# One transformer kernel on Trainium2: inverse sums turned into rows on TensorE before their store, mem's reload behind a projection's slabs, first halves that end in the order of the second, one add on VectorE

## What is computed

```python
h_res = h_res + rms_norm(m @ w_o[i], post_norm_g[i])          # end of the first block
...
h = rmsnorm(x, ln1[l]);  z = h @ w_in[l]
s = einsum('bqhd,bkhd->bhqk', qi, k) * scale                  # forgetting attention, 8 heads of 64
s = s + (ci[..., :, None] - cT[..., None, :])                 # causal, c = cumsum(log_sigmoid(f))
p = softmax(s);  fx_out = einsum('bhqk,bkhd->bqhd', p, v)
x = x + concat([ml_out, fx_out], -1) @ w_out[l]
x = x + cross_attention(rmsnorm(x, ln_x[l]), rmsnorm(mem, ln_mem[l]), w_xq[l], w_xkv[l], w_xo[l])
u = relu(rmsnorm(x, ln2[l]) @ w_ff1[l]);  x = x + (u * u) @ w_ff2[l]
return rmsnorm(x, ln_f)
```

## Time and profile before

| | us |
|---|---|
| median of 3 runs | 2868.69 (2868.45 to 2870.37) |
| the profiled execution | 2866.0 |
| its span, first to last instruction | 2864.2 |
| PE busy, share of the span | 96% |
| PEld, DVE, ACT, POOL | 79%, 36%, 32%, 20% |
| TensorE's granted clock, mean | 0.989 |
| slab to w_hi on ACT (L1357), mean | 1.055 |
| slab to w_lo on POOL (L507), mean | 2.44 |

### The profile page before, as it was taken

How to read it: one execution, slowest core, us unless ns; L and a number is a source line. 1 busy time by engine, 2 the same in 40 slices (tenths; PEclk the granted TensorE clock), 3 DMA queues, 4 the chain that set the end, 5 groups by cost and what they waited for, 6 DMA issues and landing times.

```text
span 2864.2 us, 34206 instructions
## 1 busy us (share of the span) xinstructions
PE 2762.2 (96%) x13636; PEld 2269.4 (79%) x13636; DVE 1029.4 (36%) x1292; ACT 923.6 (32%) x1469; POOL 581.4 (20%) x246
## 2 busy tenths in 40 slices
PE   7999999999999999999999998899999999999999
PEld 6677788898888887777778887677688888888887
DVE  3544423553313222734534665221323212122223
ACT  4455531112222114433435554233423112021122
POOL 1000012221222223321011224231021222222221
PEclk9899999999999999999999999899999999999999
DMA  3000001111111114121113344320020111111112
GB/s 124 14 13 13 15 22 45 52 45 44 45 44 48 48 51 147 45 91 37 37 44 74 54 84 115 112 66 30 22 66 30 52 45 51 52 44 51 44 52 88
DMA packets 50966, 154.50 MB, mean 54 GB/s; under 512 B 13140, under 2 KB 13396, under 8 KB 50088
## 3 DMA queue, kind: packets, MB, share of 16 engines
q1 hardware_dynamic: 45904, 128.11, 15.2%
q10 hardware_dynamic: 4952, 24.82, 2.3%
HBM read 138.04 MB, written 10.67 MB: 52 GB/s over the span
## 4 chain that ended last, share of the span: by engine, by line
PE 48%; issue 38%; POOL 5%; DVE 3%; ACT 2%; DMA 2%; POOLq 0%; SPq 0%; DVEq 0%; ACTq 0%
PE ps L594 19%; PE ps L675 15%; PE ps L696 4%; POOL w_lo L507 4%; PE ps L1108 2%; DMA w_raw<-in_units 2%; PE ps L1066 1%; PE ps L1257 1%; PE ps L1060 1%; DVE fx_tl L2504 1%; PE ps L1145 1%; DVE stat L2495 1%; PE ps L1282 1%; PE ps L1166 1%; ACT fx_th L1866 1%
## 5 line engine op out<-in xcount | busy, mean ns | idle before, releaser
L507 POOL TENSOR_TENSOR w_lo<-w_raw,w_hi 128x1024 fp32r<-128x1024 f32 x205 | 500.1, 2440 | 2138.8 <-ACT w_hi L1357 2138.6
L594 PE MATMUL ps<-A_hi,w_hi 128*128 128x512 f32 (+1 forms) x1920 | 549.0, 372 | 7.5 <-POOL w_lo L507 1.5
L594 PE MATMUL ps<-A_lo,w_hi 128*128 128x512 f32 (+1 forms) x1920 | 545.3, 370 | 0.0
L594 PE MATMUL ps<-A_hi,w_lo 128*128 128x512 f32 (+1 forms) x1920 | 544.5, 370 | 0.0
L594 PEld LDWEIGHTS ps<-A_hi,w_hi 128*128 128x128 f32 x1920 | 341.8, 189 | 71.5 <-issue 6.2
L594 PEld LDWEIGHTS ps<-A_hi,w_lo 128*128 128x128 f32 x1920 | 343.4, 189 | 61.8
L594 PEld LDWEIGHTS ps<-A_lo,w_hi 128*128 128x128 f32 x1920 | 343.3, 188 | 61.5
L1357 ACT ACTIVATE w_hi<-w_raw 128x1024 fp32r<-128x1024 f32 x205 | 216.2, 1055 | 517.2 <-PE ps L675 331.2
L2572 DVE TENSOR_TENSOR X<-ps,X 128x512 f32<-128x512 f32 x96 | 66.4, 692 | 394.9 <-PE ps L675 317.1
L675 PE MATMUL ps<-w_hi,U_hi 128*128 128x512 f32 x448 | 174.3, 389 | 0.0
L675 PE MATMUL ps<-w_lo,U_hi 128*128 128x512 f32 x448 | 174.3, 389 | 0.0
(11 more groups left out here) (421 smaller groups left out, 4205.7 us busy)
## 6 DMA issues: line engine op xcount, KB each, us to landing
w_raw<-in_units SPq DMA_DIRECT2D x203, 512.0 KB, 3.5
X<-in_x ACTq DMA_DIRECT2D x4, 1024.0 KB, 11.6
X<-in_x ACTq DMA_DIRECT2D x1, 4096.0 KB, 14.9
x_spill<-X ACTq DMA_DIRECT2D x1, 4096.0 KB, 12.2
X<-x_spill ACTq DMA_DIRECT2D x1, 4096.0 KB, 15.9
out<-lnf_xn SPq DMA_DIRECT2D x8, 512.0 KB, 2.6
w_raw<-in_units SPq DMA_DIRECT2D x12, 256.0 KB, 2.5
negm_bc<-negm_rows ACTq DMA_DIRECT2D x4, 512.0 KB, 3.5
```

The source lines that it names most:

```text
L507: nc.gpsimd.tensor_tensor(w_lo[:, slot, :], w_raw[:, slot, :], w_hi[:, slot, :].bitcast(F32), ALU.subtract).then_inc(w_lo_ready, 1)
L594: last = nc.tensor.matmul(out, w[:, slot, o:o + m], v[:, k, cols] if k is not None else v[:, cols], start=(first and j == 0 and q == 0), s ...
```

## The change

Five edits, and the diff's core below.

1. **Inverse sums as rows.** After the last chunk of the first step of head h+1, PE transposes head h's 128 x 8 inverse sums into free columns of that chunk's bank (fx_row_turn; for head 7 after the last step's chunks). ACT copies the 8 x 128 result to fx_row (fx_row_copy). SP stores that: 8 rows of 128 floats (inverse_out waits for fx["row"]). DVE's inverse of head h waits for the transpose of head h-2, no longer for its store.
2. **SP's order.** inverse(h) is inverse_out(h) and inverse_in(h) together; inverse(h-1) stands in head h's turn, before copies(2h+3); inverse(5) before copies(15), inverse(6) after the load of n0+13, inverse(7) after the load of n0+17. The wait for fx["out"] and the two reloads of mem move behind the loads of w_out's eighth unit.
3. **POOL's order.** normalised(6) moves between the low parts of n0+14 and n0+15.
4. **Tiles of the first halves.** The last unit (kp 3) of w_o's, w_out's and w_xo's first half goes in the order TILES, ACT and DVE read the banks in that order, and the second half's tile o waits for o + 1 banks.
5. **Last add.** For the last tile DVE adds Y to X, before its ln1 scaling of the tile before; POOL's new_x(7) goes, and ACT's last stats waits for x_last.

```diff
@@ -294,6 +294,7 @@
 fx_inv = ar("fx_inv", 79872, [P, S])
+fx_row = ar("fx_row", 83968, [P, 2, P])
@@ -364,7 +365,7 @@
 fx = {k: sem(f"fx_{k}") for k in ("half", "q_hi", "q_lo", "dup0", "dup1", "sc", "nm", "p", "t", "ph", "pl", "vh", "vl", "pv",
-                                  "o", "inv", "inv_out", "inv_in", "out", "ones")}
+                                  "o", "inv", "row", "inv_out", "inv_in", "out", "ones")}
 mem_moved = sem("mem_moved")
@@ -376,6 +377,7 @@
 y_sq, y_cp, y_std, post_g_in, x_new = sem("y_sq"), sem("y_cp"), sem("y_std"), sem("post_g_in"), sem("x_new")
+x_last = sem("x_last")
 y_new = sem("y_new")
@@ -415,9 +417,8 @@
         def inverse_out(h):
-            sp.wait_ge(fx["inv"], h + 1)
-            sp.dma_start(inv_d[h % 2].rearrange("q p -> p q"), stat[:, 16 + 8 * (h % 2):24 + 8 * (h % 2)],
-                         allow_slow_non_contiguous=True).then_inc(fx["inv_out"], 16)
+            sp.wait_ge(fx["row"], h + 1)
+            sp.dma_start(inv_d[h % 2], fx_row[0:ST, h % 2, :]).then_inc(fx["inv_out"], 16)
@@ -441,35 +442,29 @@
         sp.wait_ge(mem_moved, 32)
+        def inverse(h):
+            inverse_out(h)
+            inverse_in(h)
...
             next_load(n0 + 4 + h)
+            if h:
+                inverse(h - 1)
             copies(2 * h + 3)
-            if h:
-                inverse_in(h - 1)
             copies(2 * h + 4)
...
                 sp.dma_start(mem_lo_a.bitcast(F32), meml_d.rearrange("p (a b) c -> p a (b c)", b=2)).then_inc(mem_moved, 16)
-            inverse_out(h)
         next_load(n0 + 10)
+        inverse(5)
         copies(15)
-        inverse_in(5)
-        next_load(n0 + 11)
-        next_load(n0 + 12)
-        inverse_out(6)
-        next_load(n0 + 13)
-        next_load(n0 + 14)
-        inverse_in(6)
-        next_load(n0 + 15)
-        next_load(n0 + 16)
-        inverse_out(7)
-        next_load(n0 + 17)
-        inverse_in(7)
-        sp.wait_ge(fx["out"], HEADS)
-        sp.wait_ge(mem_moved, 64)
-        sp.dma_start(mem_hi_x[:, :, :].bitcast(F32), memh_d).then_inc(mem_moved, 16)
-        sp.dma_start(mem_lo_x[:, :, :].bitcast(F32), meml_d).then_inc(mem_moved, 16)
+        for n in range(n0 + 11, n0 + 14):
+            next_load(n)
+        inverse(6)
+        for n in range(n0 + 14, n0 + 18):
+            next_load(n)
+        inverse(7)
@@ -481,6 +476,10 @@
                 load(n, n % 2, 1024)
+            sp.wait_ge(fx["out"], HEADS)
+            sp.wait_ge(mem_moved, 64)
+            sp.dma_start(mem_hi_x[:, :, :].bitcast(F32), memh_d).then_inc(mem_moved, 16)
+            sp.dma_start(mem_lo_x[:, :, :].bitcast(F32), meml_d).then_inc(mem_moved, 16)
         elif iterations == 1:
@@ -536,7 +535,6 @@
         new_x(o)
-    new_x(ST - 1)
     b = FIRST["w_xo"] + 4
@@ -565,9 +563,11 @@
             normalised(h - 1, n0 + h + 4)
-    for n in range(n0 + 10, n0 + 18):
+    for n in range(n0 + 10, n0 + 15):
         low(n, n % 2)
-    normalised(6, n0 + 18)
+    normalised(6, n0 + 15)
+    for n in range(n0 + 15, n0 + 18):
+        low(n, n % 2)
     normalised(7, n0 + 18)
@@ -983,7 +983,7 @@
             pe.wait_ge(sp_lo, SPLIT[split] + 2 * kp + 2)
-            sweep_unit(n0 + kp, (n0 + kp) % 2, kp, hi, lo, off, tiles=tiles, free=free)
+            sweep_unit(n0 + kp, (n0 + kp) % 2, kp, hi, lo, off, tiles=TILES if kp == 3 else tiles, free=free)
@@ -1006,7 +1006,7 @@
-    sweep_tiles(n0 - 4, wo_hi, wo_lo, A_hi, A_lo, META, lambda o: pe.wait_ge(y_cp, TILES[o] + 1),
+    sweep_tiles(n0 - 4, wo_hi, wo_lo, A_hi, A_lo, META, lambda o: pe.wait_ge(y_cp, o + 1),
                 lambda o: ln1_tile(o - 3) if o >= 3 else None)
@@ -1143,7 +1143,16 @@
                 last = nc.tensor.transpose(ps[:, 4 + g % 2, x * P:(x + 1) * P], fx_p[:, o:o + P], ident)
+            if s == 0 and c == 3 and h:
+                last = fx_row_turn(h - 1, g)
             last.then_inc(fx["t"], 1)
+    def fx_row_turn(h, g):
+        e = h % 2
+        pe.wait_ge(fx["inv"], h + 1)
+        return nc.tensor.transpose(ps[0:ST, 4 + g % 2, 384:512], stat[:, 16 + 8 * e:24 + 8 * e], ident)
@@ -1214,12 +1223,15 @@
             fx_fill(4 * h + s + 1)
+    pe.wait_ge(fx["pl"], FX_CHUNKS * HEADS - 1)
+    fx_row_turn(7, FX_CHUNKS * HEADS).then_inc(fx["t"], 1)
     fx_values(7, 3)
...
             pe.wait_ge(fx["pl"], FX_CHUNKS * HEADS)
+            pe.wait_ge(fx["row"], HEADS)
         if o == 6:
@@ -1231,7 +1243,7 @@
-    sweep_tiles(FIRST["w_out"] + 4, wout_hi, wout_lo, A_hi, A_lo, META, lambda o: pe.wait_ge(sw["w_out"], TILES[o] + 1),
+    sweep_tiles(FIRST["w_out"] + 4, wout_hi, wout_lo, A_hi, A_lo, META, lambda o: pe.wait_ge(sw["w_out"], o + 1),
                 lambda o: lnx_tile(o - 3) if o >= 3 else None)
@@ -1310,7 +1322,7 @@
-    sweep_tiles(n0 - 4, wxo_hi, wxo_lo, A_hi, A_lo, META, lambda o: pe.wait_ge(sw["w_xo"], TILES[o] + 1),
+    sweep_tiles(n0 - 4, wxo_hi, wxo_lo, A_hi, A_lo, META, lambda o: pe.wait_ge(sw["w_xo"], o + 1),
                 lambda o: ln2_tile(o - 3) if o >= 3 else None)
@@ -1680,12 +1692,12 @@
     feed(n0 + 8, n0 % 2, (n0 + 8) // 2)
-    for t in range(ST):
-        take_y(0, t, t)
+    for o, t in enumerate(TILES):
+        take_y(0, o, t)
     feed(n0 + 9, (n0 + 9) % 2, (n0 + 9) // 2)
...
     ln1 = Norm("ln1", lambda t: X[:, t, :], ln1_t, A_hi, TILES, 32, META, (2, 3),
-               ready=lambda o: act.wait_ge(x_new, o + 1))
+               ready=lambda o: act.wait_ge(x_new, o + 1) if o + 1 < ST else act.wait_ge(x_last, 1))
     for o, t in enumerate(TILES):
@@ -1852,6 +1864,14 @@
+    def fx_row_copy(h, g):
+        if h == 0:
+            act.wait_ge(mem_moved, 32)
+        if h >= 2:
+            act.wait_ge(fx["inv_out"], 16 * (h - 1))
+        fn(fx_row[0:ST, h % 2, :], ps[0:ST, 4 + g % 2, 384:512], ACT.Copy).then_inc(fx["row"], 1)
@@ -1863,6 +1883,8 @@
             w = HB if c < j else 384
+            if s == 0 and c == 3 and h:
+                fx_row_copy(h - 1, g)
             fn(fx_th[:, FX_T_AT[j] + c, 0:w], ps[:, 4 + g % 2, 0:w], ACT.Copy).then_inc(fx["ph"], 1)
@@ -1908,6 +1930,8 @@
     x_key(6)
+    act.wait_ge(fx["t"], FX_CHUNKS * HEADS + 1)
+    fx_row_copy(7, FX_CHUNKS * HEADS)
     split_hi(mix, lambda k: None, range(2, 4))
@@ -2350,8 +2374,11 @@
             v.tensor_tensor(X[:, TILES[0], :], X[:, TILES[0], :], Y[:, TILES[0], :], ALU.add).then_inc(x_new, 1)
-        else:
-            ln1.xn()
+            continue
+        if o + 1 == ST:
+            dve.wait_ge(y_new, ST)
+            v.tensor_tensor(X[:, TILES[o], :], X[:, TILES[o], :], Y[:, TILES[o], :], ALU.add).then_inc(x_last, 1)
+        ln1.xn()
     ln1.xn()
@@ -2521,7 +2548,7 @@
         if h >= 2:
-            dve.wait_ge(fx["inv_out"], 16 * (h - 1))
+            dve.wait_ge(fx["t"], FX_CHUNKS * (h - 1) + 4)
         v.reciprocal(stat[:, 16 + 8 * e:24 + 8 * e], stat[:, 80 + 8 * e:88 + 8 * e]).then_inc(fx["inv"], 1)
@@ -2575,7 +2602,7 @@
     lnx = Norm("lnx", lambda t: X[:, t, :], lnx_t, A_hi, A_lo, TILES, 32, META, LNX_PAIRS)
-    residual("w_out", 0, 0, FIRST["w_out"] + 3, tiles=range(ST))
+    residual("w_out", 0, 0, FIRST["w_out"] + 3)
@@ -2615,7 +2642,7 @@
     ln2 = Norm("ln2", lambda t: X[:, t, :], ln2_t, A_hi, A_lo, TILES, 0, META, LN2_PAIRS)
-    residual("w_xo", 0, 0, FIRST["w_xo"] + 3, tiles=range(ST))
+    residual("w_xo", 0, 0, FIRST["w_xo"] + 3)
```

## The result

The changed kernel takes 2843.52 us (median, 2843.15 to 2848.60), the kernel before, run beside it, 2869.53 (2868.45 to 2872.96): a ratio of 0.991, 95% interval 0.9895 to 0.992. Forecast were 2841.5 us. The profiled execution of after takes 2843.15 us, 22.85 less than that of before; forecast for that pair were 27.2. Most terms of the sum can be read off at their size, but 4.35 us of the gain are missing.

A forecast was written before the change was run, and what follows sets the result against it. PE's waits were taken as the bound. 2866.0 (profiled) - 21.5 + 1.0 - 5.5 - 1.2 = 2838.8, plus 2.7 for the median gives 2841.5 us; range 2836 to 2852 with (a) and (b).

The forecast's parts named there:

- Bound and cause: PE's waits bound the kernel; the longest, 17.4 us for a w_out slab's low part, comes from SP's queue.
- Part 1: Tail of SP's queue: w_out's third slab loads earlier, its first half runs without the wait; gain 21.5 us (19 to 22).
- Part 2: Heads: eight added inverse-row transposes on PE, with ACT copies; 1.0 us lost (0.3 to 3.2).
- Part 3: w_o: the first half's tile order lets the second half follow at once; gain 5.5 us (bound 3 to 5.5).
- Part 4: Last add on DVE: the low part PE awaits at L617 comes earlier; gain 1.2 us (0.8 to 2.6).
- POOL's move: normalised(6) ahead of three low parts, reading SBUF beside DVE's first split of mix; nothing counted, 2.4 us more at worst.
- later stages follow PE and shift whole: Stages after the edited ones were taken to start earlier by the full gain, with no term of their own.
- (a): Rows get in the heads' way: seven heads lose 0.8 us each, x_k's seventh slab 2 us late; 2849, chance 0.09.
- (b): w_o's wait stays in part as the feed before ACT's first copy slips; 5.5 us come back, 2847, chance 0.04.
- (c): Bandwidth, not SP's order, held w_out's slab, so nothing gained there: 2863; listed as 2866 for a median, chance 0.03.
- (d): Inverse-sums store stays slow and SP holds the heads: loss begins at 8.1 to 9.4 us of store; chance 0.02.
- The signs of being wrong: A new wait over 3 us in the heads, or a held slab late at w_out's second half.

The follow-up runs named there:

- run 1: Kernel before with only SP's order changed: the wait for fx["out"] and both mem reloads behind w_out's eighth unit's load; 2855.20 us, ratio 0.995.
- run 3: Kernel before with only the order TILES in w_o's first half, last unit; 2864.39 us, ratio 0.9986.
- run 4: Kernel before with only the last add moved to DVE; 2868.73 us, ratio 0.9995.
- run 6: Changed kernel with POOL's order of before, both last products behind the low part of n0+17; 2844.02 us, ratio 0.991.
- second set: Both kernels timed and traced again, unedited: changed kernel 2846.27 us, ratio 0.992; kernel before 2871.28 us, ratio 1.0006.
- run 5: Changed kernel with the element-wise store of the inverse sums in the new place, DVE waiting for it again; 2853.20 us, ratio 0.995.

## Why the prediction was right, and where it was short

- **Bound and cause.** Right. w_out's loss came from SP's queue, three quarters of it from the order alone (run 1: 15.9 of 21.3).
- **Part 1, 21.5 forecast.** Measured 21.3 (64.85 to 43.55). The store took 2.3 us where I took 2.6 as the least, and that of head 6 only 1.2 (1730.96 to 1732.19). The Trainium skill, page DMA: Bandwidth & Descriptors, section Anatomy of one DMA — SWDGE (gpsimd) path, fits a fixed 2.0 us for DMAs issued from GpSimd; this store goes out from SP and was done in 1.2. The measurement decides, and the sum doesn't hang on it. Wrong in the working: "even with an 11.2 us store the slab lands at about 1774.7" was meant as cover. It lands, but ACT doesn't feed it before mix is split (run 1). Landing is not the last step of a slab; ACT's own order ahead of the feed had to be walked too.
- **Part 2, 1.0 lost forecast.** Measured 0.75 (226.16 to 226.91). In x_k's seventh slab and in the copies nothing was lost.
- **Part 3, 5.5 forecast.** Measured 5.5, in the changed kernel and alone (run 3), 3.76 of it to the second half's first matmul and 1.73 behind it.
- **Part 4, 1.2 forecast.** The wait is 1.2 shorter, in the changed kernel and alone (run 4). The stage's row in the table shows 0.8 and 1.4 for the changed kernel. In run 4 it shows 2.6, the upper bound of the forecast: there the clock did not fall behind the wait, as the prediction had held possible. Which of the two comes, the forecast could not tell, and the runs don't say why.
- **POOL's move, nothing forecast.** Nothing measured (run 6). The moved product took 2.37 us. DVE's first split of mix beside it took 2.02 us, 1.23 in the kernel before; the last inverse sums' transpose on PE then waited 0.1 to 0.2 us. The prediction's "2.4 us more at worst" was too low by its own numbers, which had up to 3.3 us for the product.
- **The step that failed:** "later stages follow PE and shift whole". The transposes add instructions to PE's stream; with them a packet of the instruction queue fell into the transfer of one slab, and one of the slab's sixteen shares came late. That cost 1.0 to 1.8 us in x_v and 1.5 to 1.6 of lower clock behind the longer wait, 2.6 to 3.4 us that no term held. In the profiled pair 1.6 more is the clock in the last head, and start-up gives 0.8 back. By the table: 21.3 - 0.75 + 5.5 + 0.8 - 1.7 - 1.5 - 1.6 + 0.8 = 22.85.
- **The median.** 2843.5, 2.0 over the forecast; with the second set (2846.3) it is 2 to 5 over. The loss at x_v accounts for about 3. That the first set came as near as 2.0 is partly luck: the forecast added 2.7 us because the profiled execution of the kernel before lay that much under its median, and that of the changed kernel lay only 0.4 under. In the second pair of profiled executions the gain was 28.65 us, since that of the kernel before started slowly.
- **The rivals.** (a) no: 0.75 in eight heads. (b) no. (c) refuted by run 1; its working gives 2863 (2841.5 + 21.5), and the 2866 beside its chance does not follow from it. (d) didn't occur, and run 5 shows that it was priced too high: at 10 us of store it costs 6.7 in the heads, where its own working gives 9 to 17.
- **The signs of being wrong.** None appeared: no new wait over 3 us stands in the heads, and no held slab was late at w_out's second half. None of the signs named in advance looked at a stage without an edit, where the loss was.

## What to carry to other kernels

Follow a late slab through every step to its user (issue, landing, the feeding engine's own order) before giving it cover, and price a queue's order and a slow store together, since their gains overlap. Where a kernel lives within a microsecond of a wait, instructions added to PE's stream can cost more than their own duration, far behind the place where they stand: compare the stages that the edit doesn't touch, in two traces of each kernel, and look at the instruction queue's packets.
